# In the attention, ScalarE takes the exponentials of a unit ahead of the copy of the transposed probabilities of the unit two places back

## What is computed

```python
def attend(q_blk):
    s = jnp.einsum('bqhcd,bkhcd->bhcqk', q_blk, k).astype(f32) * scale
    p = jax.nn.softmax(s, axis=-1)
    pd = p[:, :, 0] - lam * p[:, :, 1]
    return jnp.einsum('bhqk,bkhv->bqhv', pd, v32)

o = rms_norm(o, subln_w) * (1.0 - lam_init)
...
h = x + (jnp.concatenate([o_hg, o_da], axis=-1) @ w_out)
return h + expert_choice_moe(rms_norm(h, norm2_w), router_w, w1, w3, w2)
```

## Time and profile before

| | |
|---|---|
| time, median of 3 runs | 2150.53 us (2148.68 to 2152.47) |
| the profiled execution | time 2150.68 us, span 2148.9 us |
| PE busy | 2032.2 us, 95% of the span |
| DVE busy | 1605.8 us, 75% |
| ACT busy | 1344.6 us, 63% |
| POOL busy | 75.6 us, 4% |

### The profile page before, as it was taken

How to read it: one execution, slowest core, us unless ns; L and a number is a source line. 1 busy time by engine, 2 the same in 40 slices (tenths; PEclk the granted TensorE clock), 3 DMA queues, 4 the chain that set the end, 5 groups by cost and what they waited for, 6 DMA issues and landing times.

```text
span 2148.9 us, 27651 instructions
## 1 busy us (share of the span) xinstructions
PE 2032.2 (95%) x10732; PEld 1557.8 (72%) x10732; DVE 1605.8 (75%) x1099; ACT 1344.6 (63%) x1017; POOL 75.6 (4%) x38
## 2 busy tenths in 40 slices
PE   6999996778949999999999999999999999999998
PEld 5899996646737777777777777777777777777775
DVE  4245664575348888888888888888888888888886
ACT  4223331473237777777777777777777777777774
POOL 0000000000020000000000000000000000000000
PEclk9999997888979999999999999999999999999999
DMA  5212313112639999999999999999999999999994
GB/s 174 68 60 76 96 58 125 59 59 83 222 132 355 360 391 370 378 379 367 392 356 393 368 381 379 362 395 359 393 366 386 373 362 396 356 395 368 387 380 148
DMA packets 191058, 618.27 MB, mean 288 GB/s; under 512 B 12448, under 2 KB 37024, under 8 KB 191008
## 3 DMA queue, kind: packets, MB, share of 16 engines
q1 hardware_dynamic: 187424, 604.99, 75.2%
q0 software_dynamic: 3584, 12.58, 2.6%
HBM read 597.09 MB, written 20.45 MB: 287 GB/s over the span
## 4 chain that ended last, share of the span: by engine, by line
PE 73%; DVE 2%; DMA 1%; ACT 0%; issue 0%; SPq 0%; POOL 0%; ACTq 0%; DVEq 0%; POOLq 0%
PE pair L493 24%; PE pair L495 23%; PE pair L494 23%; PE pair L787 1%; DMA hg<-projected 1%; PE pair L716 1%; PE pair L739 1%; DVE top_tokens L1419 0%; DVE top_values L1417 0%; DVE affinity_t L1420 0%; PE pair L709 0%; DMA xe<-moe_rows,token 0%; DVE mixed L1370 0%; DVE mixed L1389 0%; DVE mixed L1328 0%
## 5 line engine op out<-in xcount | busy, mean ns | idle before, releaser
L1448 DVE TENSOR_TENSOR chunk_low<-ring,chunk_high 128x2048 fp32r<-128x2048 f32 (+1 forms) x382 | 1175.4, 3087 | 224.8 <-ACT chunk_high L1004 224.8
L1004 ACT ACTIVATE chunk_high<-ring 128x3072 fp32r<-128x3072 f32 (+1 forms) x384 | 979.1, 2558 | 213.8 <-PE pair L495 213.4
L493 PE MATMUL pair<-chunk_high,xe_high 128*96 128x512 f32 (+1 forms) x1536 | 579.4, 377 | 1.3 <-DVE xe_low L1442 1.3
L495 PE MATMUL pair<-chunk_high,xe_low 128*96 128x512 f32 (+1 forms) x1536 | 575.1, 374 | 0.0
L494 PE MATMUL pair<-chunk_low,xe_high 128*96 128x512 f32 (+1 forms) x1536 | 573.1, 373 | 0.0
L493 PEld LDWEIGHTS pair<-chunk_high,xe_high 128*96 128x96 f32 x1536 | 248.2, 162 | 90.0 <-DVE chunk_low L1448 2.5
L495 PEld LDWEIGHTS pair<-chunk_high,xe_low 128*96 128x96 f32 x1536 | 247.7, 161 | 90.3
L494 PEld LDWEIGHTS pair<-chunk_low,xe_high 128*96 128x96 f32 x1536 | 248.5, 162 | 87.3
L493 PE MATMUL pair<-chunk_high,hid_high 128*96 128x512 f32 x704 | 280.2, 398 | 0.0
L495 PE MATMUL pair<-chunk_high,hid_low 128*96 128x512 f32 x704 | 277.0, 393 | 0.0
L494 PE MATMUL pair<-chunk_low,hid_high 128*96 128x512 f32 x704 | 275.9, 392 | 0.0
(11 more groups left out here) (202 smaller groups left out, 1845.2 us busy)
## 6 DMA issues: line engine op xcount, KB each, us to landing
ring<-w SPq DMA_DIRECT2D x288, 1536.0 KB, 9.4
ring<-w SPq DMA_DIRECT2D x96, 1024.0 KB, 8.3
raw_w<-w_in SPq DMA_DIRECT2D x16, 1024.0 KB, 6.0
projected<-stage SPq DMA_DIRECT2D x60, 128.0 KB, 1.7
wo_raw<-w_out SPq DMA_DIRECT2D x8, 512.0 KB, 3.3
x_in<-x SPq DMA_DIRECT2D x6, 512.0 KB, 8.4
qk<-projected SPq DMA_DIRECT2D x6, 512.0 KB, 3.9
x_again<-x SPq DMA_DIRECT2D x6, 512.0 KB, 4.6
```

The source lines that it names most:

```text
L493: pe.matmul(dst, a_high, b_high, start=first, stop=False)
L495: return pe.matmul(dst, a_low, b_high, start=False, stop=last)
L1004: act.activation(ch[c % SPLIT][:, 0:n], ring[c % RING][:, 0:n], ACT.Copy).then_inc(ch_done, 1)
L1448: dve.tensor_tensor(cl[c % SPLIT][:, 0:n], ring[c % RING][:, 0:n], ch[c % SPLIT][:, 0:n].bitcast(F32), ALU.subtract).then_inc(cl_done, 1)
```

## The change

In each step of ScalarE's loop the copy of unit a-2 is moved from ahead of exp(a) to behind it. No operation is added, removed or resized, and no other engine's order changes.

```diff
         for a in range(ATT_UNITS + 4):
-            if 2 <= a < ATT_UNITS + 2:
-                evac_probs(a - 2)
             if a < ATT_UNITS:
                 n = KEY_TILES[a // HEADS] * P
                 act.wait_ge(mx_done, a + 1)
...
                 ins.then_inc(ex_done, 1)
+            if 2 <= a < ATT_UNITS + 2:
+                evac_probs(a - 2)
             if a < TILES:
                 act.wait_ge(go_mm, a + 1)
```

## The result

The changed kernel took 2155.56 us (median of 8 executions, 2153.58 to 2156.19) against 2148.3 us for the kernel before (8 executions, 2146.73 to 2152.47): a ratio of 1.003, with a 95% interval from 1.0019 to 1.0041. It is slower, by 4 to 9 us. The prediction gave 2152.8 us (2149.5 to 2156.0), so the time lies in the range. But the delay, 7.3 us here and 6.1 when repeated, is about three times the 2.25 us that were counted. That the range holds the time is partly luck: it was laid around 2150.53 us, the median of three executions, and its upper end is 5.5 us above that; the eight executions before have their median at 2148.3.

The account below looks back on a forecast made before the run. The prediction took ScalarE and VectorE in turn to bound the attention, and so the kernel. Its terms, 0.11 + 0.67 + 1.47 = 2.25 us, on the median 2150.53 gave 2152.8 us, range 2149.5 to 2156.0.

Parts of the forecast that it names:

- the circle: Attention's repeating chain of waits: squares, sumsq, max, diff, transpose, values, scores, max, diff, weights, max, exp, squares; sets its pace.
- The copies, 0.49 us in each of three tiles: Steps 12 to 15, 16 to 19, 20 to 23: one copy between exponentials and squares, +0.49 us each, 1.47 us.
- Steps 0 to 7: Attention's start: 0 in steps 0 to 6, hidden by the recurrence's matmuls; +0.11 us at step 7.
- Steps 8 to 11: Tile 1: copy(6) delays values(6), scores(10), max(10) and exp(10), another copy precedes the squares; +0.67 us.
- Step 24 and on: Attention's end: no exponentials left to pass, order as before; 0 us.
- covered with 0.1 us to spare: Behind exp(20): copy(18) ends at 482.17, before values(18) start at 482.28, so it adds no delay.
- The rival on the clock: TensorE's full clock returns later, slowing values(19) and scores(23): 3.6 us more, 2156.4 us; chance 0.06.
- No later stage has a clock of its own.: Behind the attention: no later stage would swallow the 2.25 us delay; later stages look the same, shifted.
- The copies' waits: ScalarE: copies waiting 11.5 us hold up exponentials; all regained 2139.0, part 2150.5 to 2151.5; partial or no effect 0.14.
- Nothing moves: Slack between squares and sumsq absorbs the delay: 2150.5 us; chance 0.14, shared with part of the copies' wait regained.
- That the change costs nothing measurable: Whole kernel: time stays the same within the 0.2%, 4.3 us, threshold; chance 0.91.

Follow-up runs that it names:

- the control: The kernel before, unchanged, timed and profiled again beside the kernel before: 2149.79 us against 2149.6, ratio 1.000.
- both fillings: Unused identity transposes in TensorE's gaps in attention and output projection start, against the kernel before: order of before 2145.89 us (0.9979), changed order 2148.32 us (0.9987).

## Why the prediction was right, and where it was too small

**The direction and the circle.** This part was right. That the copy costs and gives nothing back followed from where it stood: ahead of the exponentials it filled time in which ScalarE waited for the maxima; behind them it delays the squares, and sumsq on VectorE stands in front of max and diff. The rows after show it (3.46 in place of 2.97 us), and moving sumsq away took 15.5 us off the kernel.

**The copies, 0.49 us in each of three tiles.** Right to a hundredth where the clock is held: with both fillings 0.48 and 0.49 us per tile (15.93 against 15.45 and 15.44, 14.99 against 14.50). Where it isn't, the tiles scatter about that: between the first profiles of the two kernels it was 0.60, 0.31 and 0.32 us.

**Steps 0 to 7.** As forecast: the copy fits ahead of the recurrence's copy, and sumsq of tile 0 waits 3.04 us where it waited 2.93, the 0.11 counted.

**Steps 8 to 11, counted as 0.67 us.** Measured 0.90, 0.91 and 0.66 over the 18.03 of before; the chain values(6), scores(10), max(10), exp(10) is the one described. The term leaves out that values(6) and scores(10) might meet more of the half clock: they took 1.23 and 2.08 us after the change, and 1.06 and 1.98 before it. With the clock held the term is 0.26 to 0.29 us, near the 0.28 that was expected for it then.

**Step 24 and on, counted as 0.** With the clock held it is 0 (6.69 and 6.70 us for tile 5 in both orders). Without, tile 5 took 8.21, 7.85 and 7.68 us before and 8.72, 8.73 and 8.04 after, 0.6 us more on average; this is part of what hangs on the clock.

**The step that failed: copy(18), "covered with 0.1 us to spare", and with it the clock, taken as fixed.** The cover was TensorE's transposes at half clock, 0.90 us from their start to that of the values. In two of three profiles of before transpose(15) and transpose(19) ran at full clock, 0.49 us from their start to that of the values, and their tiles were 0.6 us (tile 3) and 1.1 us (tile 4) shorter. Behind the changed order values(18) wait for copy(18), which lets them start 0.85 us after the transposes, so that this gain is in part lost. How large a part can be read at max(22): from the start of transpose(19) it took 484.78 - 481.00 = 3.78 us in the control and 488.57 - 483.84 = 4.73 in the changed kernel. Of these 0.95 us, 0.35 are the later start of the values; the other 0.60 come behind it, from values and scores that met more of the half clock. In tile 2 the control gained 0.6 us with transpose(11) still at half clock (1.12 us), since scores(14) took 1.48 us in place of 2.08. The prediction took the clock of its one profile for the kernel's own.

**The rival on the clock, "0.06".** Of the rivals it came nearest, with 2156.4 us, and its chance was far too small. Its place was wrong: it looked for the cost at values(19) and scores(23), and it came at the blocks ahead of max(22). VectorE waited for scores(14), (18) and (22) together 4.65, 2.36 and 2.29 us in the three profiles of before, and 4.44, 4.74 and 4.99 in those of the changed kernel: 1.6 us more on average. The change costs 4.5 us in the attention, of which 1.85 or 1.75 are left with the clock held up, and about 5.3 us of the span. The sum of 2.25 us was met only against the profile that it was counted from: there the squares of tile 4 come 2.24 us later, counted from exp(0), with more than forecast in tiles 1 and 2 and less in tiles 3 and 4. Against the other two profiles of before they come 4.6 us later.

**"No later stage has a clock of its own."** From the squares of tile 5 to the expert rows it took 131.7 us on average in the three profiles before and 132.5 after, with 1.2 to 1.3 us of scatter in each set. Part of that is TensorE's clock again. The router's logits of the first tile, first in the profile before, then after:

```profile
585.17 1.92 PE L716 MATMUL pair<-xt_t,router_w 128*16 128x128 f32 x16
```

```profile
588.37 2.96 PE L716 MATMUL pair<-xt_t,router_w 128*16 128x128 f32 x16
```

The control has a stretch as long (132.20 us), with logits of 1.92 us, so neither the longer stretch nor the slower logits can be laid to the change.

**The rivals that fell.** The copies' waits gave nothing back. "Nothing moves" is out by the interval (its 0.02 us between squares and sumsq is 0.01 by the earlier trace rows, which changes nothing). That the change costs nothing measurable had 0.91 and should have had much less.

**What stays open.** Why the changed order had the longer attention in every profile, and whether it must. Part of it is the copy that keeps values(18) from starting early. But the kernel with the swap in the squares' steps alone, in which copy(18) isn't moved, also waited 1.55 us for its scores three times, in its one profile. That the change costs more than the 2.25 us is no chance of the profiled executions: the 18 executions of the changed kernel (8 and 10) took 2152.05 to 2156.51 us, and the 32 of before that were timed beside its repetition 2147.66 to 2152.16. Of the 6 us between the medians, 4.5 were found in the attention by the means of the profiles, and some 0.8 behind it, within its scatter.

## What to carry to other kernels

Before moving an instruction off an engine's way, look at what the engine would do in that time: a wait that only overlaps another wait is free, and behind it the same instruction may land in a stretch that has no slack. Here the cure was not on ScalarE at all but on VectorE, where a reduction that nobody needed soon stood, waiting, in front of the two operations that everybody waited for.

And a cover measured in one profile holds only for the clock that this profile met. Where a stage falls between TensorE's two clocks, take two or three profiles of the kernel before, and count each cover at both speeds.

## What was unexpected in the hardware

The same program met half clock at different blocks of the same loop in different executions: transpose(15) took 1.11 us in one profile of before and 0.66 in another, and its tile 17.08 or 16.49 us. Work that computes nothing held the clock up: transposes of the identity in TensorE's gaps, 28 of them and 3.28 us in a gap of 3.9 us, kept the granted clock at 1.00 from 425 to 497 us, and with the order of before each tile repeated to 0.01 us in a second kernel with the same filling. The Trainium skill, "TensorE: Matmul & The Clock Gate", section "Part 1: The HAM clock gate (the "warmup" mystery)", says that idleness throttles the array to half rate and activity releases it, at a point that varies from run to run. The profiles agree: from the squares of tile 0 to those of tile 5 the granted clock was 0.82, 0.84 and 0.84 in the three of before, with other blocks at half clock, and 1.00 with the gaps filled. And the saving moves on: with the attention's gaps filled, the output projection began at half clock and gave some 2 us back, until its own gaps were filled as well (first matmuls of 0.80 and 0.63 us in the profile before, 0.50 and 0.39 with the filling). The output projection's first two matmuls, before:

```profile
507.65 0.80 PE L493 MATMUL pair<-wo_high,mix_high 128*128 128x512 f32 x1 [2.05 <-DVE mix_low L1335]
508.25 0.63 PE L494 MATMUL pair<-wo_low,mix_high 128*128 128x512 f32 x1
```

and with both fillings in the order of before:

```profile
503.23 0.50 PE L493 MATMUL pair<-wo_high,mix_high 128*128 128x512 f32 x1 [1.11 <-DVE mix_low L1349]
503.57 0.39 PE L494 MATMUL pair<-wo_low,mix_high 128*128 128x512 f32 x1
```
